# Attention rewritten in straight-line code with two heads a step, masks added by TensorE

## What is computed

```python
s = einsum('qd,kd->qk', q, k) * d**-0.5          # d = 64
s = where(valid, s, -1e30)                        # window, near columns or band
p = exp(s - m); l = p.sum(-1)                     # m: row maximum (and sink)
o = (p @ v) / l                                   # sinks: l += exp(sink - m)
```

## Time and profile before

| | |
|---|---|
| median of 3 runs | 4659.3 us (4657.78 to 4667.65) |
| the profiled execution | 4661.39 us |
| its span, first to last instruction | 4659.6 us |
| mean granted TensorE clock | 0.960 of full |
| busy: PE, PEld, DVE, ACT, POOL | 92%, 86%, 68%, 39%, 1% |
| the seven attention blocks, from their first instruction to the last copied output | 323 us |

### The profile page before, as it was taken

One profiled execution on the slowest core, in us unless ns is written; L12 is line 12 of the kernel. 1 busy time (PEld: TensorE's weight loads), 2 busy tenths in 40 slices (PEclk: granted clock), 3 DMA queues, 4 the chain that ended last, 5 costly groups with the idle time before them and its releaser, 6 DMA issues. The chain is left out here.

```text
span 4659.6 us, 88155 instructions
## 1 busy us (share of the span) xinstructions
PE 4265.5 (92%) x33089; PEld 4019.9 (86%) x33098; DVE 3163.8 (68%) x5645; ACT 1833.8 (39%) x2663; POOL 49.0 (1%) x82
## 2 busy tenths in 40 slices
PE   8977999959888679999999899999988889999998
PEld 8956999849884479899999898999987589899998
DVE  5676565466524647987777588877771748887787
ACT  4424343334322334444333444443332444444333
POOL 0000000000000001000000010000000001000000
PEclk9988999979999889999999999999999999999999
DMA  6633666426421136655777475567752247556775
GB/s 229 204 129 109 222 206 227 148 66 233 150 101 46 45 109 206 194 176 179 222 229 226 152 229 177 175 191 227 229 170 75 64 150 228 175 176 192 228 227 178
DMA packets 323046, 803.61 MB, mean 172 GB/s; under 512 B 34912, under 2 KB 152672, under 8 KB 322016
## 3 DMA queue, kind: packets, MB, share of 16 engines
q1 hardware_dynamic: 322784, 800.00, 53.9%
HBM read 731.70 MB, written 51.38 MB: 168 GB/s over the span
## 5 line engine op out<-in xcount | busy, mean ns | idle before, releaser
L263 PE MATMUL banks<-h_parts,ring_hi 128*128 128x256 f32 x7920 | 1982.6, 288 | 115.8 <-ACT ring_hi L246 106.1
L246 ACT ACTIVATE ring_hi<-ring 128x1024 fp32r<-128x1024 f32 x1166 | 1234.4, 1059 | 1965.8 <-PE banks L267 1935.4
L264 PE MATMUL banks<-h_parts,ring_hi 128*128 128x256 f32 x7920 | 1959.2, 285 | 0.0
L252 DVE TENSOR_TENSOR ring_lo<-ring,ring_hi 128x1024 fp32r<-128x1024 f32 x1166 | 1427.4, 1225 | 728.5 <-ACT ring_hi L246 715.5
L263 PEld LDWEIGHTS banks<-h_parts,ring_hi 128*128 128x128 f32 x7920 | 1532.0, 193 | 130.5 <-issue 69.3
L264 PEld LDWEIGHTS banks<-h_parts,ring_hi 128*128 128x128 f32 x7920 | 1533.5, 194 | 0.3
L267 PE MATMUL banks<-h_parts,ring_lo 128*128 128x256 f32 x7920 | 1117.4, 284 | 0.8 <-DVE ring_lo L252 0.6
L267 PEld LDWEIGHTS banks<-h_parts,ring_lo 128*128 128x128 f32 x7920 | 1027.7, 193 | 2.5 <-DVE ring_lo L252 2.5
L1609 DVE TENSOR_TENSOR scratch<-con,picks 128x1024 f32<-128x1024 f32 x192 | 235.2, 1225 | 128.2 <-PE banks L1493 128.2
L263 PE MATMUL banks<-h_parts_ctx,ring_hi 128*128 128x256 f32 x992 | 245.1, 285 | 0.0
L264 PE MATMUL banks<-h_parts_ctx,ring_hi 128*128 128x256 f32 x992 | 243.1, 283 | 0.0
(11 more groups left out here) (201 smaller groups left out, 3455.3 us busy)
## 6 DMA issues: line engine op xcount, KB each, us to landing
ring<-peer_u_dram SPq DMA_DIRECT2D x384, 512.0 KB, 3.7
ring<-peer_v_dram SPq DMA_DIRECT2D x384, 512.0 KB, 3.8
act_store<-acts_out SPq DMA_DIRECT2D x384, 128.0 KB, 3.0
scratch<-act_store SPq DMA_DIRECT2D x384, 128.0 KB, 3.5
ring<-ffn_gate_dram SPq DMA_DIRECT2D x88, 512.0 KB, 3.7
ring<-ffn_up_dram SPq DMA_DIRECT2D x88, 512.0 KB, 3.5
ring<-ffn_down_dram SPq DMA_DIRECT2D x88, 512.0 KB, 3.6
big<-mod_w_dram SPq DMA_DIRECT2D x80, 512.0 KB, 4.5
```

The costliest lines, as they stand in the source:

```text
L246: self.nc.scalar.activation(self.hi[:, n % 2], self.ring[:, self.slot(j)], ACT.Copy).then_inc(self.count("tile_hi").sem, 1)
L252: self.nc.vector.tensor_tensor(self.lo[:, self.slot(j)], self.ring[:, self.slot(j)], self.hi[:, n % 2].bitcast(F32), ALU.subtract).then_in ...
L263: self.nc.tensor.matmul(out, w, b_hi, start=opens and m == 0, stop=False)
L264: self.nc.tensor.matmul(out, w, b_lo, start=False, stop=False)
```

## The change

`attention` is written anew for pairs. A pair `p` is a group `j` with a query half `t`, so both heads are handled in one step; there are 8 pairs in a block and 16 in the seventh. Everything is unrolled, so q, keys and v are read where they lie: no staging of q, keys or values, no zeroed halves. Only the bias table is still loaded.

- Scores: two products over 64 partitions each (0 to 63 and 64 to 127), into two PSUM banks. Masks are added by a further product into the same banks: identity (bfloat16) times the mask (bfloat16, `hard`), or for the dilated block the float32 identity times a float32 table that holds log(many)/SCALE (so `times` is gone, with its table). The bias is added by a product of `eight` (identity/SCALE) with the loaded table. The mask's bfloat16 copies are made by VectorE at the start of a masked block.
- VectorE: one row maximum over both banks, one shift for both heads; sum, reciprocal for both; the copy of head 1's transposed probabilities from PSUM (ScalarE keeps head 0's).
- The probabilities are no longer scaled. TensorE spreads 1/sum over partitions (`spread`: a broadcast column of `st` times the identity), ScalarE copies that to `factors`, and VectorE multiplies the output with it while copying it from PSUM.
- Differential attention scales map 1 by lambda*sum0/sum1 and adds map 0, then goes on as one map.
- Order in step i on each engine: TensorE `scores(i)`, `turn(i-1)`, `mix(i-2)`; VectorE `highest(i)`, `invert(i-1)`, `move(i-1)`, `keep(i-2)`; ScalarE `exps(i)`, `move(i-1)`, `keep_spread(i-2)`.

The core of the new functions (removed lines are those of the printed kernel; left out are semaphore declarations and totals):

```diff
+            def scores(p):
+                j, t = pairs[p]
+                pe.wait_ge(exped.sem, exped.after(2 * (p - 1)))
+                for a in range(2):
+                    rows = slice(a * HD, (a + 1) * HD)
+                    last = nc.tensor.matmul(bank(p, a), q[rows, j, t * P:(t + 1) * P], keys[rows, key(j), 0:nk], start=True,
+                                            stop=mask is None)
+                if mask is not None:
+                    pe.wait_ge(ready.sem, ready.after(3))
+                    for a in range(2):
+                        near = bank(p, a)[:, 0:T]
+                        if bias is not None:
+                            pe.wait_ge(staged[j % 2].sem, staged[j % 2].after(16 * (j // 2 + 1)))
+                            nc.tensor.matmul(near, eight, bs[:, j % 2, a, t], start=False, stop=False)
+                        last = nc.tensor.matmul(near, k.c("ident") if soft else eye, mask[:, t] if soft else hard[:, t],
+                                                start=False, stop=True)
+                last.then_inc(scored.sem, 1)
...
+            def turn(p):
+                for a in range(maps):
+                    if diff:
+                        pe.wait_ge(combined.sem, combined.after(p + 1))
+                        pe.wait_ge(moved.sem, moved.after(p))
+                    else:
+                        pe.wait_ge(exped.sem, exped.after(2 * p + a + 1))
+                        pe.wait_ge((moved, moved_too)[a].sem, (moved, moved_too)[a].after(p))
                     for b in range(nt):
...
+            def mix(p):
+                j, t = pairs[p]
+                pe.wait_ge(recip.sem, recip.after(p + 1))
+                pe.wait_ge(spread_kept.sem, spread_kept.after(p))
+                for a in range(maps):
+                    last = nc.tensor.matmul(k.ps[a * P // maps:(a + 1) * P // maps, 7, 0:P],
+                                            st[:, p % 2, INVERSE, a:a + 1].to_broadcast([P, P // maps]), k.c("ident"),
+                                            start=True, stop=True)
+                last.then_inc(spread.sem, 1)
+                pe.wait_ge(kept.sem, kept.after(p))
+                pe.wait_ge(moved.sem, moved.after(p + 1))
+                if not diff:
+                    pe.wait_ge(moved_too.sem, moved_too.after(p + 1))
+                for b in range(nt):
+                    for a in range(maps):
+                        rows = slice(a * P // maps, (a + 1) * P // maps)
+                        at = key(j) * P + a * HD
+                        last = nc.tensor.matmul(k.ps[rows, 6, 0:P], v[:, b, at:at + P // maps], pt[:, p % 2, a, b * P:(b + 1) * P],
+                                                start=b == 0, stop=b == nt - 1)
+                last.then_inc(mixed.sem, 1)
...
+            def highest(p):
...
+                nc.vector.reduce_max(s[:, MAX], k.ps[:, 2 * (p % 2):2 * (p % 2) + 2, 0:nk], AX).then_inc(peak.sem, 1)
...
+            def invert(p):
+                s = st[:, p % 2]
+                dve.wait_ge(exped.sem, exped.after(2 * p + 2))
+                dve.wait_ge(mixed.sem, mixed.after(p - 1))
...
+                nc.vector.reciprocal(s[:, INVERSE], sums).then_inc(recip.sem, 1)
+                if diff:
...
+                    nc.vector.scalar_tensor_tensor(pr[:, p % 2, 0], pr[:, p % 2, 1], s[:, MIX, 0:1], pr[:, p % 2, 0], ALU.mult,
+                                                   ALU.add).then_inc(combined.sem, 1)
...
+            def keep(p):
+                j, t = pairs[p]
+                dve.wait_ge(mixed.sem, mixed.after(p + 1))
+                dve.wait_ge(spread_kept.sem, spread_kept.after(p + 1))
+                nc.vector.tensor_tensor(out[:, j, t * P:(t + 1) * P], k.ps[:, 6, 0:P], factors[:, p % 2], ALU.mult).then_inc(kept.sem, 1)
...
+            def keep_spread(p):
+                act.wait_ge(spread.sem, spread.after(p + 1))
+                act.wait_ge(kept.sem, kept.after(p - 1))
+                nc.scalar.activation(factors[:, p % 2], k.ps[:, 7, 0:P], ACT.Copy).then_inc(spread_kept.sem, 1)
```

More of the change, by code:

```diff
@@ L118 @@
 )
-MASKS = {"window": 0, "dilated": 1, "times": 2, "near": 3, "band": 4}
+MASKS = {"window": 0, "dilated": 1, "near": 2, "band": 3}
 class Count:
@@ L1032, in rope, with attention @@
         s.ends(tiles)
[L1035 to L1047, removed]
+def attention(k, groups, shared, q, keys, v, out, scratch, nk, mask=None, soft=False, bias=None, sinks=None, diff=False):
+    nc, nt, NT = k.nc, nk // P, T // P
+    pairs = [(j, t) for j in range(groups) for t in range(NT)]
+    n, maps = len(pairs), 1 if diff else 2
@@ new lines, in _ @@
+            if mask is not None:
+                nc.vector.tensor_copy(hard, mask).then_inc(ready.sem, 1)
+                nc.vector.tensor_copy(eye, k.c("ident")).then_inc(ready.sem, 1)
+                nc.vector.tensor_scalar(eight, k.c("ident"), 1.0 / SCALE, None, ALU.mult).then_inc(ready.sem, 1)
+            for i in steps:
+                if i < n:
+                    highest(i)
+                if 0 <= i - 1 < n:
+                    invert(i - 1)
+                    if not diff:
+                        move(i - 1)
+                if 0 <= i - 2 < n:
+                    keep(i - 2)
@@ new lines, in _ @@
+            for i in steps:
+                if i < n:
+                    exps(i)
+                if 0 <= i - 1 < n:
+                    move(i - 1)
+                if 0 <= i - 2 < n:
+                    keep_spread(i - 2)
+    if bias is not None:
+        for m in range(2):
+            staged[m].ends(16 * ((groups + 1 - m) // 2))
+    if mask is not None:
+        ready.ends(3)
+    for c in (scored, peak, shift, recip, moved, mixed, kept, spread, spread_kept):
+        c.ends(n)
+    exped.ends(2 * n)
@@ L1251, in attention @@
+    turned.ends(maps * n)
+    if not diff:
+        moved_too.ends(n)
     if sinks is not None:
-        sunk.ends(U * turns)
-    if sinks is not None or times is not None:
-        total.ends(U * turns)
+        sink_ready.ends(n)
+        sunk.ends(n)
+    if sinks is not None or diff:
+        total.ends(n)
     if diff:
-        total.ends(NO * turns)
-        first.ends(NO * turns)
+        combined.ends(n)
 def convolve(k, a, val, gate, cat, scratch):
```

262 lines of the change are left out of this document (82 added, 180 removed).

## The result

The changed kernel takes 4609.6 us (median of 4 runs, 4607.9 to 4612.7), the kernel before beside it 4662.6 us (4657.8 to 4667.7): ratio 0.9887, 95% interval 0.987 to 0.9904, or 53 us faster. The forecast was 4616 us, 43 us faster, in a range from 4598 to 4652. The span of the profiled execution is 4607.6 us against 4659.6, 52.0 less.

A forecast was written before the change was run, and what follows sets the result against it. Attention blocks were taken as bound by VectorE, TensorE or loops through several engines. Blocks -30.9, starts -26.2 and clock +14 gave -43 us: 4661.4 to 4618 profiled, 4616 as median, range 4598 to 4652.

The forecast's parts named there:

- The starts: Time before each attention block's first row maximum: 15.9 us instead of 42.1 over seven blocks, without q and key transfers.
- The loop in blocks 1, 4 and 7: Row maximum, exponentials, ScalarE's copies, VectorE's output, next maximum: 2.86, 2.62 and 4.04 us a pair.
- main parts: Each attention block from first row maximum to last output copy; together 30.9 us less over the seven blocks.
- TensorE's sums in blocks 2 and 3: TensorE's own work per pair, longer there than the loop through the engines: 2.72 and 4.24 us.
- The value with no row: Two score products at 512 keys, between 0.86 and 1.73 us for a pair; 0.86 taken, as running side by side.
- Rival (a): The two score products don't run side by side in attention: 24 us more, 4640 us; chance 0.13.
- half the serial time: Price taken for mixing and spread products, which write two halves of one bank; mixing 0.88 us in block 7.
- rival (b): No products run side by side, TensorE becomes the bound everywhere: 37 us more, 4677 us, slower than before; chance 0.08.
- The chain: Blocks 5 and 6: maximum, combination, transposes, spread, mixing, next scores, next maximum; 5.22 and 3.34 us a pair.
- rival (c): The clock falls where TensorE idles, blocks 1, 4, 5 and 6: 22 us at half the time, 4638 us; chance 0.12.
- the clock's total: Loss to the lower granted clock, for some microseconds at the beginning of most blocks: +14 us over the seven.
- the removed table: One table less to load in the dilated mixer, lying beside products: priced at nothing.

The follow-up runs named there:

- e10: Changed kernel, with each attention block's first score product again waiting for DMA copies of q and keys; 4644.8 us, ratio 0.9972.
- e7: Changed kernel, with ScalarE copying the spread inverse before the probabilities, outside blocks 5 and 6; 4610.1 us, ratio 0.9897.
- e9: Changed kernel, with VectorE instead of TensorE adding the masks in blocks 1, 2 and 7; 4635.2 us, ratio 0.9954.
- e5: Changed kernel, with the mixing's loops exchanged, all products of one head before the other's; 4615.8 us, ratio 0.9909.
- e6: Changed kernel, with head 0's mask products between the two heads' scores in masked blocks; 4669.0 us, ratio 1.0021.
- e3: Changed kernel, with eight idle bfloat16 products ahead of each pair's transposes in blocks 5 and 6; 4594.2 us, ratio 0.9857.
- e11: Changed kernel, with the dilated mixer loading a second mask table that nothing reads; 4611.3 us, ratio 0.9904.
- e4: Changed kernel, with TensorE's spread one step earlier and ScalarE's copy of it before the exponentials, outside blocks 5 and 6; 4605.6 us, ratio 0.9882.
- e2: Changed kernel, with VectorE combining the pair before ahead of the new row maximum in blocks 5 and 6; 4598.9 us, ratio 0.9864.
- e12: Changed kernel; in blocks 5 and 6 VectorE combines before the maximum, ScalarE copies the spread inverse before exponentials, four idle products follow mixing; 4584.9 us, ratio 0.9844.

## Why the prediction was right, and where it was not

**The starts.** Forecast 15.9 us, measured 15.5; block 3 kept its 6.26 for the bias table, as said. e10 shows the cause: the copies alone bring 25.5 of the 26.6 us back.

**The loop in blocks 1, 4 and 7.** Forecast 2.86, 2.62 and 4.04, measured 2.77, 2.69 and 3.95, with the waits at the places named. e7 and e9 changed one link each, and the pair followed (e7 until TensorE took over). One term had no source: I took 0.24 us off for blocks without sinks, where the sink's exponential holds 0.18, and the pairs of blocks 1 and 4 differ by 0.08. The main parts of blocks 1 and 7 came out 2.2 and 3.1 us shorter than forecast.

**TensorE's sums in blocks 2 and 3.** Forecast 2.72 and 4.24, measured 2.93 and 4.46, so the forecast was 0.2 short; that TensorE binds them is shown by e5. e6 shows where one part went: a product on 64 input partitions of 512 columns holds TensorE for 1.05 us until the next kind starts, not the 0.86 + 0.1 that I had. The main parts of both blocks were right all the same (-12.6 and -4.9, against -12.6 and -5.0), the 0.2 a pair being made up by shorter beginnings and ends.

**Side by side.** The value with no row, 0.86 us for two score products, was the right end of its range (1.13 with latency for four instructions). The Trainium skill (TensorE: Matmul & The Clock Gate, Part 3, Packing small matmuls), which has slices of the input partitions run concurrently, is borne out by e6. Rival (a), 4640, was priced too low: of its 24 us 13 were for blocks 2, 3 and 7, and in e6 the steady pairs of blocks 1, 2, 3 and 7 cost 29 (part of it changes of arrangement that e6 adds), with 27 more in the starts and at the low clock, 4669 in all. For the mixing the step "half the serial time" was wrong in what it would cost to lose it: e5 shows 1.53 us for the serial order, so the halves overlap in part even then, and 1.04 with the last one's latency for the alternating one. So losing the alternating order alone would have cost less in the mixing than rival (b) had; that nothing overlaps, as (b) says, is seen in no run.

**Blocks 5 and 6, the step that was mis-sized.** I forecast +6.4 and +4.5 and charged 3 us of clock to them, 14 in all; they lost 17.9 and 11.6. The chain was right. Its length at full clock was 0.25 us short: e3 has pairs of 5.48 and 3.59 where 5.22 and 3.34 stood, 0.1 of it in the scores (1.13 for 0.86 + 0.16). Shorter beginnings and ends made up for that, and e3's main parts of 42.9 and 29.2 us stand near the 43.1 and 28.1 of the sum. What the clock took is the difference between them and the changed kernel, 54.6 - 42.9 = 11.7 and 35.2 - 29.2 = 6.1, 17.8 us. That is rival (c) in exactly these two blocks. In blocks 1 to 4 and 7 I had charged 11 us for the clock in their beginnings, of which next to nothing was lost (clocks of 0.93 to 1.00 in the rows): the sum over all of them was 5.9 us better even without that charge. So the clock's total (14 against 17.8) was near and its places were wrong. The error comes from one step: I took the low clock as something of a block's beginning, as the earlier trace rows have it, and gave its spreading in a chain where TensorE waits only 0.12.

**Term by term.** Starts 0.4 us better, blocks 1 to 4 and 7 5.9 better and 11.1 of clock not lost, blocks 5 and 6 15.6 worse (29.5 against 13.9): -44.9 in the attention where the terms gave -43. The agreement is in part two errors that cancel, and 7 of the 52 us measured have no term at all.

**Outside.** I had nothing there; the trace shows 7 us less, 4 of them in the dilated mixer's projection. Costing the removed table at nothing was right to within 1 us by e11's trace. Some 3 of the 7 us go with a higher granted clock ahead of block 2 (the rows at e11); what changed the clock, and the cause of the rest, are not found. e7 moved the time outside the attention by 3 us and e4 by 4 without touching it, and the stretch ahead of block 1, the same in every kernel here, ended anywhere from 374.1 to 380.3 us (e2). So a few microseconds of a comparison here need not be the edit's own.

## What to carry to other kernels

When a change takes work from the fullest engine, follow the queue order of every engine until the chain closes on itself: in blocks 1 and 4 to 7 the length of that loop, not the busy time of an engine, was the time of a pair, and moving a few operations in the queues (e2: 11 us; e12, with four idle products: 25) was worth as much as moving the masks to TensorE (e9: 22 us in the attention). Where TensorE stands in such a loop and mostly waits, price its links at the lower granted clock too, and try whether idle products in its waits pay. And put products that use different halves of the array next to each other: one small product between the two heads' scores cost 29 us in the steady pairs, and 59 in all with the longer starts and the low clock that came with it, more than the whole change had earned (e6).

## What the runs showed of the hardware

- Two float32 products on 64 input partitions each (partitions 0 to 63 and 64 to 127), written to different banks, take 1.13 us for 512 columns together (the changed kernel), one alone 1.12 (e6).
- Sixteen instructions of 128 columns that write two halves of a bank take 1.04 us alternating (the changed kernel) and 1.53 us one half after the other (e5); eight take 0.61 and 0.66.
- Two bfloat16 mask products of 256 columns take 0.39 us with the last one's latency and start 0.12 us apart (0.21 where a product on 64 partitions follows, e6).
- In blocks 5 and 6, where TensorE waited for VectorE in every pair (2.65 us of 7.08 in block 5, 1.85 in block 6), the granted clock fell to 0.50 (the lower of its levels, 1.2 GHz) again and again within the block, and the mean was 0.72 and 0.66; with idle products in the waits it stayed at 1.00 (2.4 GHz), and the kernel was 15 us faster (e3). The Trainium skill (TensorE: Matmul & The Clock Gate, Part 1: The HAM clock gate) has the clock lowered after TensorE was idle. The direction agrees, and these rows show what it costs in a chain; TensorE was not idle for long here, though, but worked in every pair between its waits.
